# Score pairs, later masks and two reordered engine queues in a two-block fp32 transformer kernel

## What is computed

```python
# block 1: differential attention, 8 heads, two score maps each
sc = einsum('bhcqd,bhckd->bhcqk', qb, k) * scale          # c: 2 maps
sc = where(dist >= 0, sc - slopes * abs(dist), -inf)
p = softmax(sc); a = p[:, :, 0] - lam * p[:, :, 1]
o = einsum('bhqk,bhkd->bhqd', a, v)
y_b = rmsnorm(o, sub_norm_g) * (1.0 - lam_init)
merged = g_a * (y_a @ w_up_a) + g_b * (y_b @ w_up_b)      # g_a, g_b = sigmoid(h @ w_gate + b_gate)
x = x + merged @ w_out                                    # then a hierarchical mixture of experts
# block 2: three branches, gated by gm = sigmoid(g_merge), and a feed-forward part
o = g0 * attend(compressed) + g1 * attend(selected) + g2 * attend(window)   # sparse attention
u = silu(layer_norm(conv31(a * sigmoid(ag))))             # convolution
o_m = softmax(qm @ km * scale) @ vm                       # attention to 256 memory tokens
```

## Time and profile before

| | us |
|---|---|
| median of three runs | 1777.59 (1775.76 to 1777.69) |
| profiled execution | 1779.48 |
| its span in the profile | 1777.9 |
| mean granted TensorE clock | 0.993 of full |
| busy: PE, DVE, POOL, ACT | 1747.7, 871.2, 750.7, 583.0 |

### The profile page before, as it was taken

One profiled execution on the slowest core, in us unless ns is written; L12 is line 12 of the kernel. 1 busy time (PEld: TensorE's weight loads), 2 busy tenths in 40 slices (PEclk: granted clock), 3 DMA queues, 4 the chain that ended last, 5 costly groups with the idle time before them and its releaser, 6 DMA issues.

```text
span 1777.9 us, 22880 instructions
## 1 busy us (share of the span) xinstructions
PE 1747.7 (98%) x8545; PEld 1305.9 (73%) x8545; DVE 871.2 (49%) x1314; ACT 583.0 (33%) x1092; POOL 750.7 (42%) x623
## 2 busy tenths in 40 slices
PE   9999999999999999999999999999999999999999
PEld 6888877777787444443688877777788788888887
DVE  4221786666663244332551688887876532112211
ACT  2313445455233111111231345554462222212220
POOL 4454443434441000000341686777845454444452
PEclk9999999999999999999899999999999999999999
DMA  6323332225343899999731522222264233333321
GB/s 228 106 77 92 93 91 81 89 72 166 95 154 124 316 381 375 385 405 380 289 92 52 178 89 72 72 75 75 83 226 127 92 95 95 98 95 95 104 84 48
DMA packets 82935, 264.25 MB, mean 149 GB/s; under 512 B 9360, under 2 KB 10384, under 8 KB 82832
## 3 DMA queue, kind: packets, MB, share of 16 engines
q1 hardware_dynamic: 64608, 230.31, 38.5%
q10 hardware_dynamic: 15920, 28.32, 4.5%
q0 software_dynamic: 2304, 4.20, 0.6%
HBM read 249.16 MB, written 17.83 MB: 150 GB/s over the span
## 4 chain that ended last, share of the span: by engine, by line
PE 93%; DVE 5%; DMA 1%; ACT 1%; issue 0%; POOL 0%; ACTq 0%; DVEq 0%; SPq 0%; POOLq 0%
PE psum L654 89%; PE psum L1443 1%; PE psum L1058 1%; DVE area_r L2127 1%; DMA more<-stream 1%; DVE area L2184 1%; PE psum L786 1%; DVE area L2763 1%; DVE area_r L2126 0%; DVE area L2243 0%; DVE root L2168 0%; PE psum L1166 0%; ACT area L1612 0%; ACT root L1612 0%; DVE root L2333 0%
## 5 line engine op out<-in xcount | busy, mean ns | idle before, releaser
L654 PE MATMUL psum<-area_r,ring_hi 128*128 128x512 f32 x3104 | 974.4, 395 | 8.0 <-ACT root L1612 4.7
L529 POOL TENSOR_TENSOR ring_lo<-ring,ring_hi 128x512 fp32r<-128x512 f32 x420 | 568.3, 1376 | 775.6 <-ACT ring_hi L1612 770.6
L654 PEld LDWEIGHTS psum<-area_r,ring_hi 128*128 128x128 f32 x3104 | 577.5, 189 | 133.7 <-issue 17.2
L654 PE MATMUL psum<-area_r,ring_lo 128*128 128x512 f32 x1552 | 606.9, 391 | 0.0
L1612 ACT ACTIVATE ring_hi<-ring 128x1024 fp32r<-128x1024 f32 x210 | 221.5, 1058 | 551.9 <-PE psum L654 516.3
L654 PEld LDWEIGHTS psum<-area_r,ring_lo 128*128 128x128 f32 x1552 | 292.3, 188 | 62.7
L1612 ACT ACTIVATE area<-psum 128x512 f32<-128x512 f32 (+3 forms) x252 | 124.0, 518 | 209.8 <-PE psum L786 60.4
L654 PE MATMUL psum<-ring,area 128*64 128x512 f32 (+1 forms) x464 | 129.9, 600 | 2.3 <-issue 1.8
L654 PE MATMUL psum<-area 128*64 128x128 f32 (+8 forms) x880 | 115.6, 342 | 2.3 <-DVE area L2169 0.8
L2127 DVE TENSOR_TENSOR area_r<-area,area_r 128x512 fp32r<-128x512 f32 x82 | 99.3, 1211 | 2.8
L585 POOL DMA_INDIRECT area<-tokens,idx x16 | 16.1, 1009 | 195.8 <-DVE idx L2491 150.2
(11 more groups left out here) (248 smaller groups left out, 1586.2 us busy)
## 6 DMA issues: line engine op xcount, KB each, us to landing
ring<-stream SPq DMA_DIRECT2D x320, 512.0 KB, 3.7
more<-stream SPq DMA_DIRECT2D x48, 1024.0 KB, 8.3
gates<-root ACTq DMA_DIRECT2D x24, 256.0 KB, 2.0
area<-gates SPq DMA_DIRECT2D x24, 256.0 KB, 5.1
gates<-area ACTq DMA_DIRECT2D x20, 256.0 KB, 4.2
area<-gates ACTq DMA_DIRECT2D x20, 256.0 KB, 5.2
area<-xT SPq DMA_DIRECT2D x8, 256.0 KB, 4.2
area<-xT ACTq DMA_DIRECT2D x8, 256.0 KB, 3.2
```

The costliest lines, as they stand in the source:

```text
L529: ins = nc.gpsimd.tensor_tensor(ring_lo[:, c % RS, n], ring[:, c % R, n], ring_hi[:, c % RS, n].bitcast(F32), ALU.subtract)
L654: return nc.tensor.matmul(out, lhsT, rhs, start=first, stop=last)
```

## The change

Four places are reordered. Each engine executes the same operations as before.

1. *Diff attention, PE.* From unit 2 on, the scores of units u and u+1 are made together in even iterations, four score matmuls and then four `slopes` matmuls (`diff_scores`). Odd iterations have no scores.
2. *Merge 1, DVE and PE.* DVE scales heads 0 to 3, gates tile 3, splits head 0, scales heads 4 to 7, and then splits heads 1 to 7 with gated tiles between. PE's second half waits for all scaling (its banks) and then for one split head at a time.
3. *Sparse attention, PE.* The query blocks go 1, 3, 0, 2 instead of 0 to 3; the masks are made by `nsa_masks`, behind the value products and ahead of the gate groups. The waits on `nov` follow the unit's number.
4. *Mem attention, ACT.* A gate tile's copy stands in the iteration that fills it, ahead of the exp; the weight copy that it releases (`follow`) comes an iteration later, and the transfer to memory as before.

```diff
-        NSA_UNITS = [(j, i) for j in range(4) for i in range(NT)]
+        NSA_UNITS = [(j, i) for j in range(4) for i in (1, 3, 0, 2)]
...
+            def diff_scores(us):
+                two = [(x, m) + score_items("diff")[0][x] for x in us for m in (0, 1)]
+                for x, m, h, i in two:
+                    t = 2 * x + m
+                    q, k, n = att_map("diff", h, i, m)
+                    if t >= 4:
+                        pe.wait_ge(S("de"), t - 3)
+                    mm(psum[:, t % 4, 0:n], q, k, True, False)
+                for x, m, h, i in two:
+                    n = P * (i + 1)
+                    mm(psum[:, (2 * x + m) % 4, 0:n], slopes[:, h, :], dist[:, 512 - n:512], False, True).then_inc(
+                        S("ds"), 1)
...
+                        if kind == "diff":
+                            if u < 2:
+                                diff_scores((u,))
+                            elif u % 2 == 0:
+                                diff_scores((u, u + 1))
...
-            pe.wait_ge(S("onout"), 16)
-            for m in range(KD):
+            pe.wait_ge(S("on_norm"), 8)
+            by_tile(C0["merge1"] + KD, 4, waited(YBH, YBL, S("onout"), 8, True))
+            for m in range(1, KD):
...
                         mm(psum[:, 2 * mi + g, 0:n], q, k, True, False)
+            def nsa_masks(u):
+                i = NSA_UNITS[u][1]
                 for mi in range(2):
                     for g in range(2):
-                        ins = mm(psum[:, 2 * mi + g, n - P:n], slopes[:, 0, :], diagbig[:], False, True)
+                        ins = mm(psum[:, 2 * mi + g, P * i:P * i + P], slopes[:, 0, :], diagbig[:], False, True)
                     ins.then_inc(S("ns"), 1)
...
-                if i == 0 and j:
+                if u % NT == 0 and j:
                     pe.wait_ge(S("nov"), j)
...
                 if u >= 2:
                     nsa_values(u - 2)
                 if u < len(NSA_UNITS):
+                    nsa_masks(u)
                     gate2(G2_NSA + u, (0, 1, 2, 3))
...
                 A(root[:, n % 2, :], psum[:, 7, :], ACT.Copy).then_inc(S("gate_raw"), 1)
-                follow(C0["gate2"] + n + 1)
+                if n < G2_MEM:
+                    follow(C0["gate2"] + n + 1)
...
-            attention("mem", fill=gate2_mem)
+            def gate2_made(u):
+                if u in MEM_FILLED:
+                    gate2_out(G2_MEM + MEM_FILLED.index(u))
+            def gate2_next(u):
+                if u - 1 in MEM_FILLED:
+                    follow(C0["gate2"] + G2_MEM + MEM_FILLED.index(u - 1) + 1)
+                if u - 2 in MEM_FILLED:
+                    gate2_keep(G2_MEM + MEM_FILLED.index(u - 2))
+            attention("mem", fill=gate2_next, made=gate2_made)
...
             for m in range(3):
                 gated(0, m)
+            for h in range(4):
+                head_scaled(h)
+            gated(0, 3)
+            head_split(0)
+            for h in range(4, 8):
+                head_scaled(h)
+            for h in range(1, 8):
+                head_split(h)
+                if h % 2 and h > 1:
+                    gated(0, 4 + h // 2 - 1)
+            gated(0, KD - 1)
```

More of the change, by code:

```diff
@@ L759, in attention @@
                     if u < len(units):
[L760 to L768, removed]
-                        if kind == "diff":
-                            for t in (2 * u, 2 * u + 1):
-                                mm(psum[:, t % 4, 0:n], slopes[:, h, :], dist[:, 512 - n:512], False, True).then_inc(
-                                    S("ds"), 1)
+                        if kind == "diff":
+                            if u < 2:
+                                diff_scores((u,))
+                            elif u % 2 == 0:
+                                diff_scores((u, u + 1))
+                        else:
+                            h, i = units[u]
+                            q, k, n = att_map(kind, h, i, 0)
+                            if u >= 4:
+                                pe.wait_ge(S("me"), u - 3)
+                            mm(psum[:, u % 4, 0:n], q, k, True, True).then_inc(S("ms"), 1)
                         if fill is not None:
@@ L1668, in normed, with attention @@
                             between(j)
-            def attention(kind, fill=None):
+            def attention(kind, fill=None, made=None):
                 units, maps = score_items(kind)
@@ L1675, in attention @@
                         fill(u)
+                    if made is not None:
+                        made(u)
                     if u < len(units):
@@ L2046, in _ @@
                         A(p, p, ACT.Exp, negm[:, col + 4 + g:col + 5 + g], 1.0).then_inc(S("ne"), 1)
-                if u >= 2 and NSA_UNITS[u - 2][1] == NT - 1:
+                if u >= 2 and (u - 2) % NT == NT - 1:
                     act.wait_ge(S("no"), u - 1)
                     A(tile(OUT["nsa"][NSA_UNITS[u - 2][0]]), psum[:, 6, :], ACT.Copy).then_inc(S("nov"), 1)
[L2051 to L2058, removed]
-            attention("mem", fill=gate2_mem)
+            MEM_FILLED = [max(q for q in range(4 * NT) if MEM_FILL[q][0] == x) for x in range(3 * KD - G2_MEM)]
+            def gate2_made(u):
[7 more added lines that the diff above has]
+            attention("mem", fill=gate2_next, made=gate2_made)
             act.wait_ge(S("mt"), 16)
@@ L2339, in gated, with head_scaled @@
                 V.tensor_tensor(t, t, psum[:, 4 * j + m % 4, :], ALU.mult).then_inc(S("bank_read"), 1)
-            for m in range(3):
-                gated(0, m)
-            for h in range(8):
+            def head_scaled(h):
                 dve.wait_ge(S("on_bc"), h + 1)
@@ L2346, in _, with head_split @@
                                        op0=ALU.mult, op1=ALU.mult).then_inc(S("on_norm"), 1)
+            def head_split(h):
                 dve.wait_ge(S("on_norm"), h + 1)
                 split(tr(YBH + h), tr(YBL + h), tile(Q + h)).then_inc(S("onout"), 1)
-            for m in range(3, KD):
+            for m in range(3):
                 gated(0, m)
+            for h in range(4):
[9 more added lines that the diff above has]
+            gated(0, KD - 1)
             for m in range(KD):
```

## The result

The change takes 1779.72 us (median of 20 runs, 1776.74 to 1782.14), the kernel before 1776.82 (20 runs, 1773.34 to 1780.58): ratio 1.0013, 95% interval 1.0007 to 1.0018. That is 2.3 us by the ratio and 2.9 by the medians, inside the 0.2% of the forecast, on its slow side; the interval does not hold 1, so the small loss is real.

The account below looks back on a forecast made before the run. The prediction took the kernel to be bound by TensorE (PE), whose chain fills 93% of the span. Its terms, -6.2 + 9.9 - 0.2 - 3.5, summed to 0.0, so 1777.6 us, own range 1774 to 1781.2, 8-in-10 range 1769 to 1785.5.

Parts of the forecast that it names:

- merge: Merge 1, PE and DVE: without PE's stall on head scaling 4.2 us gained, and 2.0 from the clock; gain 6.2.
- diff attention: PE: pairing scores uncovers ACT's gate copy; 1.09 us lost in each of 6 pairs, 0.45 in 7; sum +9.9.
- sparse attention: PE: masks beside the gate -2.8 us, three waits on the output bank's copy +2.2, first units +0.4; net -0.2.
- mem attention: ACT: gate copy ahead of the exp removes most of PE's 4.7 us of waits; gain 3.5, ends 1.5 and 4.5.
- The saving of 0.49 a pair: Diff attention, PE: a pair saves one entry into scores (0.21), one into slopes (0.14) and one coming from value products (0.14).
- The faster rival: Diff attention: gate copy runs ahead of other copies, PE does not stand; part -4.3, total 1763.4 us; side's chance 0.30.
- the dearer case: Merge: all of DVE's splits contend with POOL; DVE ends 5.0 us late and 1.2 of the gain is left.
- The 2.0 us of clock: Merge: the lower granted clock behind PE's stall loses 2.0 us; without the stall the clock stays up.
- the 0.4 booked for the first units: Sparse attention, PE: the first units, without values to cover them, may lose 0.4 us.
- The slower rival: Sparse attention: late masks make compressed scores wait; +8 us, 1785.6; chance 0.26, including diff stalls at their upper end.
- the 0.8 booked as waits coming back: Mem attention: about 0.8 us of the removed waits return as waits on exps or transposed copies.
- The signs: Profile: no scaling wait; 13 or 14 diff waits, some 14 us; three sparse near 0.7, none at compressed scores; mem about 1.2.

Follow-up runs that it names:

- e6: The change with the mem attention's gate copy put back behind the exp and the transposed copy; 1783.12 us, one run.
- e2: The change with ACT copying the diff attention's gate bank one step earlier, ahead of its other copies; 1765.72 us, ratio 0.9936 to the kernel before.
- e4: The change with the query blocks in their old order 0, 1, 2, 3, masks still beside the gate; 1779.99 us, one run.
- e10: The change with both sparse edits undone: masks ahead of the value products, blocks 0, 1, 2, 3; 1780.73 us, one run.
- e11: The change itself, unedited, run again for a second profile; 1779.23 us, one run.
- e7: The change with the merge's old order put back, DVE scaling and splitting head by head; 1785.29 us, one run.
- e0: The kernel before, unedited, run again for a second profile; 1778.77 us, one run.

## Why the prediction was right, by its own steps

**The sum** said no change, and it is 0.13%. Its terms against the marks:

| term | forecast | measured |
|---|---|---|
| merge | -6.2 | -4.2 to -6.6 |
| diff attention | +9.9 (ends +6, +12) | +12.0 to +12.3 |
| sparse attention | -0.2 | -0.2 (e6) |
| mem attention | -3.5 | -4.0 |
| sum | 0.0 | +1.4 to +3.7 by the marks, +2.3 to +2.9 by the times |

The mechanism of each term is the one forecast. That the sum came so near is in part luck: the diff term was over 2 us too small, and by the marks of the first profiles merge and mem gave 0.9 of that back.

**Diff attention.** The mechanism is as forecast: ACT's gate copy, last behind value products, 14 waits and some 14 us of standing. The term was short by 2.1 to 2.4, so the measured cost lies at or just above its upper end. The standing was sized right. Its cost is the difference between the change and e2 by the marks, 1.49 in a wide pair, exactly as forecast; the timeline prints 1.27, because it counts from the modelled end of the last value product, 0.2 behind the point at which its successor starts. In a narrow pair it is 0.70, and 0.93 with the 0.23 that e2 still has, for a forecast of 0.86, or 0.94 with the 0.08 of restart. What pairing takes away between value products and gate was right too, 1.74 by the marks for a forecast of 1.77, but that "coming from value products costs some 0.14 more" no row shows; the starts before give 0.09.

The saving of 0.49 a pair was the mis-sized part. It is 0.45 in a wide pair, where the 0.08 booked for a restart, which no row shows, made up for it: 1.09 was forecast, 1.04 to 1.10 measured. In a narrow pair it is 0.36, so that 0.54 to 0.60 was lost instead of 0.45, 1 us over seven. The first pair cost 1.46 and not 0.69: its 512 wide scores took 1.51 from the first start to the slopes, where those of the next wide pair took 0.96, and why is open. The last lost 0.2 where I had booked a gain of 0.48: the last score pair has no gate behind it, and PE waited 0.47 for ACT's transposed copy instead.

**The faster rival** gave the right condition and too large a price: with the gate copy first in ACT's queue (e2) the part gained 2.2, not 4.3. The wide pairs gained 2.7, the narrow ones 0.9 since ACT still held them a little, and the first and the last pair cost 1.4, where the rival counted them as gains.

**Merge.** Both places as forecast: no stall, clock up, and the splits in time. Only two of the eight subtractions met POOL, and took 1.67 and not 0.69; the dearer case, by the rule of "SBUF — State Buffer" in the Trainium skill, had all of them. The rule is borne out, and how often it applied decided. The 2.0 us of clock were one draw: 1.2 less in the second profile of before.

**Sparse attention.** The net of -0.2 came out, with -2.1 where -2.8 was forecast (e4 against e10) and +1.9 where +2.2 (the change against e4); with the 0.4 booked for the first units, which waited less and not more (0.61, where before had 0.82 and 0.89), the agreement of the net is partly luck. What the text did not say is that masks and order are bound to each other: the masks were the cover for the output bank's copy. The slower rival, late masks that starve the compressed scores, did not occur at a 512 wide unit in any of the ten profiles with late masks; the cover was enough, even by so little. There the second exp ends 0.28 to 0.32 ahead of the compressed scores (1085.94 and 1086.22 in e4), and where PE was held by it, at the third unit, 0.14; so some 0.15 was left (an estimate from the two), where the forecast had 0.1. A wait on exps stood at the third unit alone, 0.91 in e4 and 0.15 in e11.

**Mem attention.** -4.0 for -3.5: of the 0.8 booked as waits coming back, two small ones came (0.22 and 0.48).

**The signs.** Fourteen waits of 13.5 us in the diff part, three of 0.66 in the sparse part, none on scaling and none at the compressed scores were as foretold; seven of the fourteen were 0.71, just under the 0.8 named, and the mem waits were 1.05 for 1.2.

## What to carry to other kernels

When work is moved away from between a producer and a wait, list what the next engine has to do in that gap, in its queue's order: here two copies stood behind the value products for 1.09 us, and the last was the one waited for. Moving that copy to the moment when its bank fills cost nothing and turned a loss of 12 us into a gain of 2. And two edits that touch the same gap have to be costed together: masks that leave it and narrow scores that enter it took away the cover twice.

## What the runs showed that I had not expected

**One operation, two durations, by who starts first.** DVE's subtraction in the split of the norm (8 rows of 512) and POOL's weight split start at almost the same time at the merge. In the change:

```profile
447.61 0.68 DVE L2153 TENSOR_TENSOR root_r<-root,root_r 8x512 fp32r<-8x512 f32 x1
```

```profile
447.88 1.57 POOL L529 TENSOR_TENSOR ring_lo<-ring,ring_hi 128x512 fp32r<-128x512 f32 x1 [4.71 <-ACT ring_hi L1630]
```

and in e2:

```profile
434.48 3.00 POOL L529 TENSOR_TENSOR ring_lo<-ring,ring_hi 128x512 fp32r<-128x512 f32 x2 [4.38 <-ACT ring_hi L1630]
```

```profile
434.49 1.83 DVE L2159 TENSOR_TENSOR root_r<-root,root_r 8x512 fp32r<-8x512 f32 x1
```

Begun 0.27 us ahead of POOL it takes 0.68; begun 0.01 behind, 1.83, and PE waits 1.00 for it. Four of the fourteen profiles have the long one (1.66 to 1.83, with PE waits of 0.82 to 1.00: e2, e4, e7 and e11, which is the change itself), the other ten 0.68. In the four DVE began 0.01 to 0.18 behind POOL, in the ten 0.15 to 0.87 ahead of it. POOL's start follows ACT's weight copy, and that follows the landing of a gate tile from memory, for which ACT waited 0.47 in the change and 0.18 in e2. "SBUF — State Buffer" in the Trainium skill, Who interferes with whom, says that the order of issue decides who blocks, and all fourteen profiles agree. For a reader of profiles it is a coin of 1.1 us that no edit tossed; e0 shows 1.2 in the same stretch from the clock alone.

**The clock behind a stall differs between executions of one program**: in the two profiles of before it is at half for 6.8 and 3.4 us at the merge, and for 10.2 and 3.4 us near 880. A span from one profile carries an error of 1 to 3 us from this, as much as the whole change makes; marks at the same matmul in two timelines do not, as long as the stretch between them holds no stall.
